# Depthwise convolution on token pairs: half as many columns per matmul, shifted copies by way of DRAM

## The reference

```python
u = rms_norm(h, norm_mix_g) @ w_in
c_val, c_gate, q, k, v, g, gate_lr = split(u)      # 512 512 256 256 512 512 16
# conv group, 512 channels: GLU, causal depthwise conv of width 31, LayerNorm over channels, swish
t = c_val * sigmoid(c_gate)
y = conv_general_dilated(t, conv_w, padding=(30, 0), groups=512) + conv_b
y_conv = silu(layer_norm(y) * ln_g + ln_b)
# gated linear attention, 4 heads, per-head RMSNorm, output gate silu(g)
y_gla = gla_group(q, k, v, g, gate_lr, ...)
h = h + concat[y_conv, y_gla] @ w_out
h = h + (silu(x @ w_gate) * (x @ w_up)) @ w_down   # x = rms_norm(h), width 2816
out = rms_norm(h, norm_final_g)
```

## Time and profile before

| | |
|---|---|
| median of 3 runs | 1581.4 us (1578.93 to 1582.05) |
| the profiled execution | 1586.72 us |
| its span, slowest core (7) | 1585.1 us |
| spans of the eight cores | 1560.1 to 1585.1 us |
| PE busy | 1480.6 us, 8162 matmuls |
| DVE, ACT, POOL busy | 799.1, 528.1, 230.1 us |
| DMA | 290.82 MB, 131384 packets |

### The profile page before, as it was taken

How to read it: one execution, slowest core, us unless ns; L and a number is a source line. 1 busy time by engine, 2 the same in 40 slices (tenths; PEclk the granted TensorE clock), 3 DMA queues, 4 the chain that set the end, 5 groups by cost and what they waited for, 6 DMA issues and landing times.

```text
span 1585.1 us, 26425 instructions; the slowest of 8 cores (1560.1 to 1585.1 us)
## 1 busy us (share of the span) xinstructions
PE 1480.6 (93%) x8162; PEld 681.0 (43%) x8162; DVE 799.1 (50%) x1704; ACT 528.1 (33%) x820; POOL 230.1 (15%) x294
## 2 busy tenths in 40 slices
PE   3867899999999999999999899999999999999994
PEld 1433344444444444444444344444444444444442
DVE  4557347525565247544484255643475444744323
ACT  3526342424324343314522044222533145211101
POOL 2024041103300032000400014000320003000000
PEclk9988899999999999999999999999999999999998
DMA  9966487899768873587636974469634974366551
GB/s 192 285 173 163 114 182 172 196 239 266 193 184 207 236 226 120 161 202 211 202 132 166 196 238 162 146 184 219 226 123 158 219 208 148 120 189 179 191 159 54
DMA packets 131384, 290.82 MB, mean 183 GB/s; under 512 B 50592, under 2 KB 67360, under 8 KB 131248
## 3 DMA queue, kind: packets, MB, share of 16 engines
q1 hardware_dynamic: 75664, 216.19, 44.4%
q0 software_dynamic: 17568, 63.51, 18.5%
q10 hardware_dynamic: 38016, 9.44, 4.3%
HBM read 254.16 MB, written 41.94 MB: 187 GB/s over the span
## 4 chain that ended last, share of the span: by engine, by line
PE 69%; DMA 12%; SPq 7%; issue 4%; DVE 3%; ACT 3%; POOL 1%; ACTq 1%; DVEq 0%; POOLq 0%
PE ps L643 54%; PE ps L1204 9%; SPq L769 5%; DMA xT<-xn_tm 3%; PE ps L820 3%; DMA h<-wpack 2%; DMA out<-h 2%; DMA wring<-wpack 2%; ACT yT L611 2%; DMA wring<-wsc 1%; DMA wsc<-wring 1%; SPq L437 1%; DVE xn_tm L619 1%; PE ps L632 1%; SPq L447 0%
## 5 line engine op out<-in xcount | busy, mean ns | idle before, releaser
L643 PE MATMUL ps<-x2T,wring 128*128 128x512 bf16 x2816 | 639.0, 380 | 12.7 <-DMA wring<-wsc 11.3
L643 PEld LDWEIGHTS ps<-x2T,wring 128*128 128x128 bf16 x2816 | 271.9, 98 | 348.2 <-issue 32.7
L1204 PE MATMUL ps<-wring,actT 128*128 128x512 bf16 x1408 | 311.5, 379 | 0.3 <-DMA wring<-wsc 0.2
L1188 DVE SCALAR_TENSOR_TENSOR ftmp<-ftmp,ps 128x512 f32<-128x512 f32 x176 | 119.9, 684 | 267.3 <-ACT ftmp L1187 265.0
L1187 ACT ACTIVATE ftmp<-ps 128x512 f32<-128x512 f32 x176 | 104.9, 596 | 348.7 <-PE ps L643 337.5
L1204 PEld LDWEIGHTS ps<-wring,actT 128*128 128x128 bf16 x1408 | 136.8, 98 | 167.6 <-issue 7.2
L643 PE MATMUL ps<-xT,wring 128*128 128x512 bf16 x736 | 171.4, 389 | 10.2 <-DMA xT<-xn_tm 10.2
L1190 DVE SCALAR_TENSOR_TENSOR actT<-ftmp,ps 128x512 bf16<-128x512 f32 x176 | 119.9, 685 | 39.6 <-PE ps L643 36.6
L643 PE MATMUL ps<-wring,xT 128*128 128x512 bf16 x512 | 125.0, 390 | 9.3 <-DMA wring<-wpack 8.0
L643 PE MATMUL ps<-wring,yT 128*128 128x512 bf16 x512 | 121.2, 389 | 2.0 <-ACT x2T L635 1.3
L643 PEld LDWEIGHTS ps<-xT,wring 128*128 128x128 bf16 x736 | 72.7, 100 | 99.5 <-issue 20.3
(11 more groups left out here) (176 smaller groups left out, 1245.9 us busy)
## 6 DMA issues: line engine op xcount, KB each, us to landing
wring<-wsc SPq DMA_DIRECT2D x319, 512.0 KB, 4.8
wring<-wpack POOLq DMA_DIRECT2D x63, 512.0 KB, 8.2
wsc<-wring SPq DMA_DIRECT2D x46, 512.0 KB, 6.3
rep<-vT SPq DMA_DIRECT2D x256, 67.5 KB, 5.5
h<-xin POOLq DMA_DIRECT2D x28, 512.0 KB, 10.8
out<-h POOLq DMA_DIRECT2D x28, 512.0 KB, 6.8
h<-xin SPq DMA_DIRECT2D x4, 512.0 KB, 12.6
out<-h SPq DMA_DIRECT2D x4, 512.0 KB, 2.6
```

The source lines that it names most:

```text
L643: ins = e.matmul(pt_ap, lhsT=lhs(kc), rhs=rhs(kc), start=(kc == 0), stop=(kc == KC - 1))
L1188: P.add("dve", lambda e: e.scalar_tensor_tensor(out=th[:], in0=th[:], scalar=1.0, in1=pg[:], op0=ALU.add, op1=ALU.mult), R=[Bpg, Bth], W=[ ...
L1204: ins = e.matmul(ps[t][:], lhsT=actT[:, j, t * 128:(t + 1) * 128], rhs=wd3[:, j - j0, :], start=(j == 0), stop=(j == NJ - 1))
```

## The change

**Pairs of tokens.** Tokens are stored in another order: in each tile of 128, first the 64 even ones, then the 64 odd ones (the host permutes the input and permutes the output back). `vT[:, c]` holds the even and the odd tokens of a block as two rows of 16 + 256 elements. The convolution now computes two neighbouring tokens ("phases") at once: a matmul's 128 partitions are 16 channels by 8 shifts, its 32 outputs are 16 channels by 2 phases, and its columns are the 256 pairs. A chunk of 128 channels is 8 groups of 16 and has 4 matmuls per group: 32 matmuls of 256 columns, into the two halves of a PSUM bank. `conv_w4` carries the taps laid out for this.

**Copies.** A DMA can't take 128 channels apart into 16 by 8 with a shift on the SBUF side, so `vT` is first stored to a scratch in DRAM (`vsc`, one DMA per chunk), and 8 DMAs per pair of chunks load `rep` from it.

**Results.** They come as (channel, phase) on partitions. The matrix of ones becomes `par`, which sums over partitions of the same phase. Each ScalarE instruction on conv results becomes two of half the size (the bias is another for each half). In block 0 the GpSimdE operations of chunks 1 and 3 go to VectorE. The last VectorE operation writes `ysq`, and four DMAs per pair of chunks sort it into `yT`, where the conv part then holds even and odd tokens apart. The output projection has, for the conv part, two matmuls of 64 output rows per channel chunk (even, odd tokens) for one of 128 (`mm_out`). The attention reads its cumulative decay in true order (`timed`, `halves`) and its mask is permuted.

**Order of block 0.** Its conv units come first, its output gates last, and the convolution stands ahead of `o0`. The gains of the later norms are loaded later.

```diff
-ORDER = (("start xt0 v0 g0 xt1 v1 g1 xt2 v2 g2 xt3 v3 g3 mt vm z decay c0 c1 rep0 c2 c3 rep1 km k q",
-          "ktr sc0 kv sc1 conv0 o0 conv1 o1 conv2 conv3 ln y0 o2 y1 ln0 o3 y2 ln1 y3 ln2 ln3 "
+ORDER = (("start xt0 xt1 xt2 xt3 mt c0 c1 rep0 c2 c3 rep1 z decay v0 v1 v2 v3 vm km k q g0 g1 g2 g3",
+          "ktr sc0 kv sc1 conv0 conv1 conv2 conv3 ln o0 o1 y0 gains o2 y1 ln0 o3 y2 ln1 y3 ln2 ln3 "
...
-                        for s_ in range(4):
-                            for g in range(4):
-                                P.add("sp", lambda e, s_=s_, g=g, c0=c - 1: e.dma_start(
-                                    out=rep[s_ * 32:(s_ + 1) * 32, c0:c0 + 2, g, :],
-                                    in_=vT[g * 32:(g + 1) * 32, c0:c0 + 2, 2 + s_:2 + s_ + 28 + T]),
...
+                        for k in (c - 1, c):
+                            P.add("sp", lambda e, k=k: e.dma_start(out=src[:, k].rearrange("q g n -> g q n"),
+                                                                   in_=vT[:, k].rearrange("p a n -> p (a n)")),
+                                  R=[BvT[k], Bhist[k]], W=[Bv[k - c + 1]], dkey=f"vs{bi % 2}_{k}")
+                        rows = src[:, cs].rearrange("q c g n -> q (c g) n")
+                        for s_ in range(8):
+                            n0 = (s_ % 2) * (16 + HT) + 4 - s_ // 2
+                            P.add("sp", lambda e, s_=s_, n0=n0: e.dma_start(
+                                out=rep[s_ * 16:(s_ + 1) * 16, cs].rearrange("p c g n -> p (c g) n"), in_=rows[:, :, n0:n0 + 12 + HT]),
...
-                            for a in range(8):
-                                for g in range(4):
-                                    ins = e.matmul(pcv[g * 32:(g + 1) * 32, :], lhsT=wcv[:, c, g, a, :],
-                                                   rhs=rep[:, c, g, 4 * a:4 * a + T], start=(a == 0), stop=(a == 7))
+                            for r in range(2):
+                                for w in range(4):
+                                    for q in range(4):
+                                        ins = e.matmul(pcv[q * 32:(q + 1) * 32, r * HT:(r + 1) * HT], lhsT=wcv[:, c, r * 4 + q, w, :],
+                                                       rhs=rep[:, c, r * 4 + q, 12 - 4 * w:12 - 4 * w + HT], start=(w == 0),
+                                                       stop=(w == 3))
...
-                        for c in range(4):
-                            ins = e.matmul(p2[:], lhsT=ones_bf[:], rhs=ysq[c], start=(c == 0), stop=(c == 3))
+                        for c in range(8):
+                            ins = e.matmul(p2[:, 0:HT], lhsT=par_bf[:], rhs=ysq[c // 2][:, (c % 2) * HT:(c % 2 + 1) * HT],
+                                           start=(c == 0), stop=(c == 7))
...
-                    P.add("pe", lambda e: e.matmul(p1[:], lhsT=ones[:], rhs=mu[:], start=True, stop=True), R=[Bmu, Bc], W=[Bp1])
+                    P.add("pe", lambda e: e.matmul(p1[:, 0:HT], lhsT=par[:], rhs=ms, start=True, stop=True), R=[Bmu, Bpar], W=[Bp1])
...
-                    P.add("dve", lambda e: e.scalar_tensor_tensor(out=yT[:, c, :], in0=yth[c], scalar=1.0, in1=y, op0=ALU.add,
-                                                                  op1=ALU.mult), R=[Bysq[c], Bycv[c]], W=[ByTc[c]])
+                    P.add("dve", lambda e: e.scalar_tensor_tensor(out=ysq[c], in0=yth[c], scalar=1.0, in1=y, op0=ALU.add,
+                                                                  op1=ALU.mult), R=[Bycv[c]], W=[Bysq[c]])
+                    if c % 2 == 1:
...
+                                P.add("sp", lambda e, r=r, a=a: e.dma_start(
+                                    out=yT[r * 64:(r + 1) * 64, cs, a * HT:(a + 1) * HT], in_=yo[a::2, :, r * HT:(r + 1) * HT]),
...
+                def mm_out(pt, t, ws):
+                    def f(e):
+                        for kc in range(4):
+                            for a in range(2):
+                                e.matmul(pt[a * 64:(a + 1) * 64, :], lhsT=yT[:, kc, a * HT + t * 64:a * HT + t * 64 + 64],
+                                         rhs=ws[0][:, kc, :], start=(kc == 0), stop=False, skip_group_check=True)
+                        ins = None
+                        for kc in range(4):
+                            ins = e.matmul(pt[:], lhsT=yT[:, 4 + kc, t * 128:(t + 1) * 128], rhs=ws[1][:, kc, :], start=False,
+                                           stop=(kc == 3), skip_group_check=True)
+                        return ins
+                    return f
```

223 lines of the change are left out of this document (137 added, 86 removed).

## The result

The changed kernel is slower: 1624.3 and 1628.5 us in the runs compared, against a median of 1580.7 for the kernel before; ratio 1.029, 95% interval 1.026 to 1.032. I had forecast 1559. The time lies outside my range and on the other side, close to the 1620 of the first rival. (Comparisons leave out the executions in which the cores of one die run at a lower clock.)

A forecast was written before the change was run, and what follows sets the result against it. TensorE was taken to bound the kernel, 98% busy in the steady part. Steady blocks -16 us and start-up -6 make -22, from a median of 1581.4 to 1559 us; range 1551 to 1584, or 1540 with free tiling changes.

The forecast's parts named there:

- the first rival: SyncE's queue before each convolution: slower copy issues delay weight loads, 61 us of waits, giving 1620; chance 0.14.
- The convolution's matmuls: Blocks 1 to 7: 256-column matmuls cost half of 512-column ones, saving 3.46 us per block.
- the rule cited ahead: Skill's rule: column tiling disables Fast Weight Load; four 32-column loads last 107 ns, as long as their four matmuls.
- LayerNorm sums and output units: Per block: halved fp32 ones matmul saves 0.44 us; tiling changes in eight output-projection units cost 1.6 us.
- Steady blocks, -2.3 us each: Blocks 1 to 7: -3.46 - 0.44 + 1.6 = -2.3 us per block, -16 us in all.
- (a) of "what lies beside other work": Steady blocks' two-hop shifted copies: two 5.5 us landings and 16 issues fit in 35.7 us, some 15 spare.
- The start-up, -6 us: Block 0's new order: convolution ends near 95 us, output projection starts at 134.5 for 141.9, less 1.6 for tiling changes.
- VectorE's idle stretch: Block 0: VectorE's 13.9 us idle in one wait for TensorE, up to 118.8 us, goes away.

The follow-up runs named there:

- n5: Changed kernel with n1's estimate and the conv half of each output unit as four full 128-column matmuls instead of eight of 64 rows: ratio 1.0040.
- n9: Changed kernel with VectorE writing the convolution's result straight into yT, without the 64 sorting DMAs: ratio 1.0167.
- n11: Changed kernel with n1's estimate and paired output units from block 1 on, and one semaphore per four yT copies: ratio 0.9964, 1577.7 us.
- n1: Changed kernel with two planner latencies raised (store landing 8 us later, vT 4 us later), so copies stand later in SyncE's order: ratio 1.0115.
- n10: Changed kernel in its own order, each rep load carrying half (128 pieces of 536 B for 256) from block 1 on: ratio 1.0024.
- n8: Changed kernel with scratch stores and rep loads of blocks 3 to 7 issued by GpSimdE instead of SyncE: ratio 1.0191.
- n2: Changed kernel whose rep loads from block 1 on read scratch nobody writes, so no wait for the store's landing; order changed too: ratio 1.0398.
- n12: Changed kernel with the rep loads halved in block 0 alone: ratio 1.0204.
- n3: Kernel before, with only the changed kernel's block 0 order and the weight rings that go with it: ratio 1.0008.

## Why the prediction was wrong, step by step

- **The convolution's matmuls: right.** 0.98 us per chunk (0.95 to 1.0 forecast), busy 36.0 us at the top of 31 to 36. Without the 0.11 of leaving that is 108 ns for four matmuls, the time of their columns. So the weight loads are hidden behind the matmuls. Whether they take the 107 ns of the rule cited ahead can't be told from this, since the columns take as long.
- **LayerNorm sums and output units: right, nearly.** A unit costs 0.22 us more, n5 prices it at 1.9 per block for my 1.6. A wait of 0.4 to 0.6 us ahead of each block's first output unit, listed above as "issue", was not in the sum. It is there with full matmuls too (n5), and gone without the `yT` copies (n9) and with one semaphore for each four of them (n11), so it goes with the wait for these eight DMAs.
- **Steady blocks, -2.3 us each: right only where nothing waits.** The shortest block went from 178.5 to 177.8, with n1's estimate to 177.1; -3.4 for the convolution, -0.4, +1.9 and +0.5 for the wait make -1.4. n10, with the same matmuls and hardly a wait, has -2.3 in the mean, of which 0.5 is less waiting and less lost clock than before. In the changed kernel the mean is +4.9, times four, and +6.5 for block 1.
- **The step that failed is (a) of "what lies beside other work"**: "the bytes are the same, in pieces of 536 B for 1080", priced by two landings of 5.5 us and an issue of 0.59. I took the landing and the issue of the old form, and asked only whether the data come in time for the convolution, which they did. The engines' time was a term put at nothing: it is 17.5 us per block for 9.2, in a stretch where weight tiles are used every 3.45 us and had 5.6 us of slack. What came of it is 3.7 us more of waiting for weights per block, and 2.3 more of lost clock, which no term of mine had. The earlier trace rows showed a DMA share of 0.68 there, as a mean over blocks; the copies fall into some 35 us of each. The loads that end the waits show that this, and not the queue's stand as such, makes most of the weights late (109 of 157 us, and 13.1 us to land), and n10, n8 and n2 agree.
- **Rival 1 had the place and nearly the price** (SyncE's queue, before the convolution; 1620) at a chance of 0.14, by the wrong mechanism: an issue costs 0.3 to 0.4 us, not more, as long as the engines are free. That its number is so near the measured time is luck. It is 61 us of waits less 22 of gain; the waits for weights grew by 17.5 us, and the start-up, 6 of the gain, became 11 of loss.
- **The start-up, -6 us: wrong, +11.** TensorE reached the key transposes at 81 us on cores 1 and 3, as forecast. I had the loads issued by 85 and the convolution done near 95. They were issued by 87.6 on core 1, 95.4 on core 3, and landed 11 to 17 us later. Halving the amount copied gives back 4.9 of the 11 (n12), leaving out the `yT` copies 5.3 (n9), for which I took one landing of 5.5 and which took 8 to 12 with four issues. VectorE's idle stretch, my lead, was replaced by two others (6.99 and 8.13 us on core 3); and n3 shows that in the kernel before an early convolution brings nothing, since block 1's tokens come next.

What stays open: what a run would give in which the queue does not stand and the order stays (n1 and n2 change it), so the division above, a third and two thirds, is read from traces and not from a time. Open too is why a read of 536 B from the scratch takes as long as 1080 B between SBUF rows. No run had pieces that start at an aligned address, or more bytes in one.

## What to carry to other kernels

Cost a rearranged copy by its packets times the time of one, over the 16 engines, and set it beside what else must land in that stretch, even when it has tens of microseconds of cover itself: the one that is late is a neighbour. A planner's order is only as good as its latencies; two numbers brought back six microseconds per block. And price a wait of TensorE with the clock that it costs behind it. When a matmul form is bracketed by changes of tiling, put several of them side by side.
